# Norm gains of the three head groups folded into the rows of the output matrix, and gates loaded from DRAM into a buffer of their own

## The chip, the cores and the metric

One core of one Trainium2 chip runs the kernel. The metric is the device time of one launch in microseconds (us). In the profile, PE is TensorE, ACT is ScalarE, DVE is VectorE, POOL is GpSimd, and SP is SyncE, which here issues nearly all transfers.

## The reference, cut to what matters

A decoder layer on 1024 tokens of width 1024. Three head groups read one input projection: stick-breaking attention (4 heads x 64), gated DeltaNet (4 x 128, in chunks) and HGRN2 (4 x 64). Their outputs are normalised per head, two of them are gated, and all go through one output projection:

```
sb_o = rms_norm(sb_o, sb_gain)
dn_o = rms_norm(dn_o, dn_gain) * silu(split_heads(dn_z, DN_HEADS))
hg_o = rms_norm(hg_o, hg_gain) * sigmoid(split_heads(hg_g, HG_HEADS))
mix = concatenate([sb_o, dn_o, hg_o])          # widths 256, 512, 256
x = x + mix @ w_out
h2 = rms_norm(x, norm2)
ff = silu(h2 @ w_gate) * (h2 @ w_up)
return rms_norm(x + ff @ w_down, final_norm)
```

Each gain multiplies a column of `mix`, and a column of `mix` meets one row of `w_out`. All is float32; a product is three matmuls of high and low halves (high x high, low x high, high x low).

## The kernel before

The program is written by hand for each engine. Every engine has one list of instructions that it works off in order; semaphores (`wait_ge`, `then_inc`, and `reach`, which waits only for a positive count) join the lists. It has four parts: norm and first projections (to about 70 us), projection beside attention (to about 460 us), the mixer in steps t = 0 to 8 over chunks of 128 tokens (about 460 to 645 us), and output projection and feed-forward (to the end).

In step t of the mixer each engine works on several chunks: t (state, scores, outputs), u = t+1 (the inverse of a triangular matrix in seven levels, and the HGRN2 decays), v = t+2 (first products) and s = t-1 (transposes of finished rows). The places that matter:

- `gates` (POOL, L1996) multiplies the activated gates in `pb` by the gain row into `gate`, two instructions for each chunk, in front of `from_start` and `values` (both recorded at L1973, as most of POOL's work, the ten `spread` instructions too). `causal` begins POOL's next step and waits for DVE's `scores`.
- `final_sb`, `final_dn`, `final_hg` (DVE, recorded in the helper `final`, L1833) write `mix` by four instructions each: length factor times gate or gain. `queries(u, 0..6)`, `scores`, the adds of `update` and `low` are recorded at L1718, `with_decay` at L1820, `log_sigmoids` at L1769, `residual` at L1724, the two scans of `running` at L1779.
- `out_high` (ACT, L662) and `out_low` (POOL, L667) split a quarter of half of `w_out` into high and low halves. The first four (n = 0) stand at the end of steps 0 to 3, the other four (n = 1) behind the mixer. `inverse(u, lv)` (ACT, L1542) copies each turned level for PE's `update` (L1270).
- On PE: `turn` L1257, `pack` L1242, `new_values` L1326, `state_update` L1354, `key_key` L1376, `gated_out` L1396 and L1399, `key_query` L1383, `m_turn` L1408, `key_state` L1282, `out_product` L2107 to L2109.
- On SP, `load_rest(t)` brings a row block of 1280 columns (gates, HGRN2 values, attention output) into `pb`; `load_keys` and `load_queries` of chunk v stand behind it.

Of the kernel before, what the change touches and what calls it, by code (L numbers as in the profile page):

```python
# [13 lines left out]
P = 128  # L14
# [6 lines left out]
def trunk_program(nc, a, out):  # L21
# [91 lines left out]
    with ExitStack() as ctx:  # L113
# [27 lines left out]
        gain_row = sb("gain_row", [P, D])  # L141
        ssq = sb("ssq", [P, NT])
# [115 lines left out]
        pb = carve(TM - 2 * DNW)  # L258
        hv = pb[:, I_AT - 2 * DNW:I_AT - 2 * DNW + HGW]
# [21 lines left out]
        for name in """rows_loaded gains_loaded o_stored0 o_stored1 gr_loaded pa_loaded pb_loaded kt_loaded0 kt_loaded1 qt_loaded hin_loaded0 hin_loaded1  # L281
# [4 lines left out]
                qd at vb gated h_dl t_init qb h_bk kd  # L286
# [372 lines left out]
        def out_high(e, n, j):  # L659
            half, at = j // 2, 2 * (j % 2)  # L660
            e.wait_ge(sems["raw_loaded1" if half else "w_loaded0"], 16 * (len(ROWS) + n + 1 if half else (W_OUT + 1) // 2 + n + 1))
            e.activation(OUT_H[n][half][:, at:at + 2, :], OUT_RAW[half][:, at:at + 2, :], ACT.Copy).then_inc(sems["wh_ready"], 1)  # L662
# [495 lines left out]
        def mixer_sync(e):  # L1158
# [10 lines left out]
            def load_rest(c):  # L1169
                reach(e, "ho_done", c)  # L1170
                reach(e, "hs_done", c)
                reach(e, "gated", c)
                reach(e, "fin_sb", c)
                e.dma_start(pb[:, :], tm_dram[c * P:(c + 1) * P, 2 * DNW:]).then_inc(sems["pb_loaded"], 16)
# [39 lines left out]
            for t in range(NT + 1):  # L1214
# [5 lines left out]
                if live(t):  # L1220
                    load_rest(t)
                if t in (4, 5):
                    load_out(e, 1, t - 4)
# [316 lines left out]
        def mixer_act(e):  # L1540
# [102 lines left out]
            def step(t):  # L1643
# [11 lines left out]
                if live(u):  # L1655
                    inverse(u, 1)
                if live(u):
# [25 lines left out]
                if 0 <= t < 4:  # L1683
                    out_high(e, 0, t)
# [31 lines left out]
        def mixer_dve(e):  # L1716
# [120 lines left out]
            def final_dn(c):  # L1837
                e.wait_ge(sems["dn_r"], 2 * c + 2)
                e.wait_ge(sems["gated"], c + 1)
# [3 lines left out]
            def final_hg(c):  # L1843
                e.wait_ge(sems["hg_r"], 2 * c + 2)
                e.wait_ge(sems["gated"], c + 1)
# [3 lines left out]
            def final_sb(c):  # L1849
# [3 lines left out]
                final(c, SBH, pb[:, SB_AT - 2 * DNW:], r_sb[:, c, :], SBD, 0, gain_row[:, 0:SBW], "fin_sb")  # L1853
# [112 lines left out]
            e.wait_ge(sems["gains_loaded"], 16 * (SBH + DNH + 4))  # L1966
# [4 lines left out]
        def mixer_pool(e):  # L1971
# [17 lines left out]

            def gates(c):  # L1990
                e.wait_ge(sems["pb_loaded"], 16 * (c + 1))
                reach(e, "fin_hg", c)
                reach(e, "fin_dn", c)
                for at_, n in ((0, DNW), (DNW, HGW)):
                    src = pb[:, (Z_AT if at_ == 0 else G_AT) - 2 * DNW:]
                    ins = e.tensor_tensor(gate[:, at_:at_ + n], src[:, 0:n], gain_row[:, SBW + at_:SBW + at_ + n], ALU.mult)  # L1996
                ins.then_inc(sems["gated"], 1)
# [37 lines left out]
            def step(t):  # L2035
# [15 lines left out]
                if live(t):  # L2051
                    gates(t)
# [834 lines left out]
```

## Time and profile before

| | us |
|---|---|
| three runs | 1378.54, 1380.06, 1381.33 (median 1380.06) |
| the profiled execution | 1376.71 |
| its span | 1375.0 |
| PE busy | 1327.3 (97%) |
| DVE, POOL, ACT busy | 783.0, 674.8, 591.7 |

The span is the time from first to last instruction in the profile. Busy times overlap; which of them sets the end is read stage by stage.

### The profile page before, as it was taken

The page shows a single profiled execution, that of the slowest core. Times are in us where ns is not written, and L with a number is a line of the kernel's source. Part 1 is how long each engine was busy: PE and PEld are TensorE (multiplying, and loading weights), DVE is VectorE, ACT ScalarE, POOL GpSimd, SP SyncE. Part 2 cuts the span into 40 slices and gives each one's busy share as a digit, 9 for nine tenths or more (in the row PEclk, how much of TensorE's full clock was granted, in tenths as well). Part 3 has the DMA queues.
Part 4 walks back from the last instruction along what each step waited for, and adds up shares of the span by engine and source line. Part 5 has one row for each costly group of instructions (what it writes and reads, how often), then busy time and mean ns, then how long its engine had stood idle before and what let it go on. Part 6 is the DMA issues. An engine that isn't in the chain of part 4 may idle for free.

```text
span 1375.0 us, 24260 instructions
## 1 busy us (share of the span) xinstructions
PE 1327.3 (97%) x9101; PEld 1102.2 (80%) x9101; DVE 783.0 (57%) x1171; ACT 591.7 (43%) x1403; POOL 674.8 (49%) x583
## 2 busy tenths in 40 slices
PE   5999999999999888989999999999999999999997
PEld 4777887988878777777888788888888888888886
DVE  5014635557364588894148855555555556665657
ACT  6234445445343567552134333333333334444445
POOL 3234324143252577750401877667666677754442
PEclk9999999999999999989999999999999999999999
DMA  5131222323224433514200344445455445876663
GB/s 185 33 102 55 89 71 87 119 74 105 78 68 123 142 120 99 181 49 158 76 17 1 108 153 149 151 151 166 150 176 176 146 146 209 324 258 195 196 188 123
DMA packets 160371, 178.60 MB, mean 130 GB/s; under 512 B 9520, under 2 KB 110464, under 8 KB 160256
## 3 DMA queue, kind: packets, MB, share of 16 engines
q1 hardware_dynamic: 160112, 176.53, 40.4%
q8 instruction: 74, 1.21, 0.4%
q10 hardware_dynamic: 144, 0.52, 0.2%
q14 instruction: 41, 0.34, 0.1%
HBM read 124.32 MB, written 52.71 MB: 129 GB/s over the span
## 4 chain that ended last, share of the span: by engine, by line
PE 83%; DVE 5%; issue 3%; POOL 3%; ACT 3%; DMA 1%; SPq 0%; DVEq 0%; POOLq 0%; ACTq 0%
PE banks L2415 9%; PE banks L2416 9%; PE banks L2417 9%; PE banks L353 6%; PE banks L355 6%; PE banks L354 6%; PE banks L2426 4%; PE banks L2427 4%; PE banks L2428 4%; PE banks L692 2%; PE banks L693 2%; PE banks L694 2%; PE banks L2107 2%; PE banks L2109 2%; PE banks L2108 2%
## 5 line engine op out<-in xcount | busy, mean ns | idle before, releaser
L2573 POOL TENSOR_TENSOR w_l<-area,w_h 128x512 fp32r<-128x512 f32 x119 | 175.6, 1481 | 180.0 <-ACT w_h L2468 135.0
L2573 POOL TENSOR_TENSOR w_l<-w_raw,w_h 128x512 fp32r<-128x512 f32 x100 | 140.5, 1405 | 99.7 <-ACT w_h L2523 50.1
L353 PE MATMUL banks<-act_h,w_h 128*128 128x512 f32 x352 | 141.3, 402 | 0.0
L355 PE MATMUL banks<-act_h,w_l 128*128 128x512 f32 x352 | 137.5, 391 | 0.0
L354 PE MATMUL banks<-act_l,w_h 128*128 128x512 f32 x352 | 137.2, 390 | 0.0
L341 POOL TENSOR_TENSOR w_l<-w_raw,w_h 128x1024 fp32r<-128x1024 f32 x24 | 59.4, 2477 | 142.3 <-ACT w_h L334 125.1
L2415 PE MATMUL banks<-act_h,w_h 128*128 128x512 f32 x320 | 124.5, 389 | 0.0
L2416 PE MATMUL banks<-act_l,w_h 128*128 128x512 f32 x320 | 124.5, 389 | 0.0
L2417 PE MATMUL banks<-act_h,w_l 128*128 128x512 f32 x320 | 124.5, 389 | 0.0
L2426 PE MATMUL banks<-w_h,act_h 128*128 128x512 f32 x308 | 120.0, 390 | 0.3 <-DVE act_l L2725 0.3
L2428 PE MATMUL banks<-w_h,act_l 128*128 128x512 f32 x308 | 119.8, 389 | 0.0
L2427 PE MATMUL banks<-w_l,act_h 128*128 128x512 f32 x308 | 119.8, 389 | 0.0
L1018 POOL TENSOR_TENSOR area<-area 128x512 f32<-128x512 f32 (+3 forms) x48 | 50.4, 1050 | 109.8 <-DVE area L1037 109.8
L2415 PE MATMUL banks<-turns,w_h 128*128 128x512 f32 x240 | 93.5, 390 | 1.3 <-POOL w_l L2573 1.3
L2416 PE MATMUL banks<-turns,w_h 128*128 128x512 f32 x240 | 93.4, 389 | 0.0
L2417 PE MATMUL banks<-turns,w_l 128*128 128x512 f32 x240 | 93.4, 389 | 0.0
L1037 DVE TENSOR_TENSOR_SCAN area<-area,zeros 128x512 f32<-128x512 f32 (+3 forms) x48 | 53.3, 1110 | 68.2 <-ACT area L934 68.2
L1973 POOL TENSOR_TENSOR area<-area 128x128 f32<-128x128 f32 (+2 forms) x144 | 72.5, 533 | 38.5 <-ACT area L1542 17.1
L2725 DVE TENSOR_TENSOR act_l<-act_h 128x512 fp32r<-128x512 f32 x40 | 56.1, 1406 | 45.2 <-ACT act_h L2526 45.2
L2468 ACT ACTIVATE w_h<-area 128x512 fp32r<-128x512 f32 x84 | 52.4, 626 | 62.4 <-PE banks L2417 28.8
L353 PEld LDWEIGHTS banks<-act_h,w_h 128*128 128x128 f32 x352 | 66.1, 188 | 15.8 <-issue 2.8
L355 PEld LDWEIGHTS banks<-act_h,w_l 128*128 128x128 f32 x352 | 66.1, 188 | 14.3
(316 smaller groups left out, 3333.2 us busy)
## 6 DMA issues: line engine op xcount, KB each, us to landing
w_raw<-in_w_in SPq DMA_DIRECT2D x22, 512.0 KB, 4.1
w_raw<-in_w_gate SPq DMA_DIRECT2D x22, 512.0 KB, 4.6
area<-in_w_up SPq DMA_DIRECT2D x22, 512.0 KB, 4.7
ff_wide<-in_w_down SPq DMA_DIRECT2D x22, 512.0 KB, 4.3
down_sums<-ff_wide SPq DMA_DIRECT2D x11, 1024.0 KB, 4.1
area<-in_x SPq DMA_DIRECT2D x8, 1024.0 KB, 7.9
projected_tm<-area SPq DMA_DIRECT2D x32, 256.0 KB, 2.3
hidden_sums<-area SPq DMA_DIRECT2D x6, 1024.0 KB, 4.2
```

The source lines that it names most:

```text
L341: e.tensor_tensor(w_l[:, b], w_raw[:, b], w_h[:, b].bitcast(F32), ALU.subtract).then_inc(sems["wl_ready"], 1)
L353: e.matmul(dst, w_h[:, b, k], act_h[:, k, cols], start=(k == 0), stop=False)
L354: e.matmul(dst, w_h[:, b, k], act_l[:, k, cols], start=False, stop=False)
L355: mm = e.matmul(dst, w_l[:, b, k], act_h[:, k, cols], start=False, stop=(k == KT - 1))
L1973: e.tensor_tensor(dst, x, y, op).then_inc(sems[name], 1)
L2415: e.matmul(dst, slot(w_h, u)[:, k], hi[:, k, :], start=(opens and k == 0), stop=False, skip_group_check=True)
L2416: e.matmul(dst, slot(w_h, u)[:, k], lo[:, k, :], start=False, stop=False, skip_group_check=True)
L2417: mm = e.matmul(dst, slot(w_l, u)[:, k], hi[:, k, :], start=False, stop=(k == 3), skip_group_check=True)
L2426: e.matmul(dst, h, slot(w_h, u), start=(k == 0 and name not in ("p6", "p5", "p3")), stop=False, skip_group_check=True)
L2427: e.matmul(dst, h, slot(w_l, u), start=False, stop=False, skip_group_check=True)
L2428: return e.matmul(dst, l, slot(w_h, u), start=False, stop=(k == PAIRS - 1), skip_group_check=True)
L2573: e.tensor_tensor(slot(w_l, u), raw_use(u) if u < NU_FF else wd_raw(u - NU_FF), slot(w_h, u).bitcast(F32), ALU.subtract).then_inc(sems["fl ...
```

## The change

The four instructions of `final_sb` become one product with the length factors alone. POOL's `gates` go; `final_dn` and `final_hg` read a `gate` buffer that SP fills from DRAM by a transfer of its own, once both have finished with the chunk before. The gains are loaded as three columns with one value for each row of `w_out` (5 small transfers in place of 12), and `out_high` multiplies its two row blocks by them in place, one ACT instruction each, before it takes the high half. For n = 0 it moves from the end of the step to between `inverse(u, 1)` and `inverse(u, 2)`.

```diff
         def out_high(e, n, j):
...
+            if n == 0 and j == 0:
+                e.wait_ge(sems["gains_loaded"], 16 * (P // SBD + 1 + P // HGD))
+            for k in (at, at + 1):
+                first = (4 * half + k) * P
+                col = 0 if first < SBW else 1 if first < SBW + DNW else 2
+                ins = e.activation(OUT_RAW[half][:, k, :], OUT_RAW[half][:, k, :], ACT.Copy, scale=gain_cols[:, col:col + 1])
+            ins.then_inc(sems["w_scaled"], 1)
+            e.wait_ge(sems["w_scaled"], 4 * n + j + 1)
             e.activation(OUT_H[n][half][:, at:at + 2, :], OUT_RAW[half][:, at:at + 2, :], ACT.Copy).then_inc(sems["wh_ready"], 1)
...
             def load_rest(c):
                 reach(e, "ho_done", c)
                 reach(e, "hs_done", c)
-                reach(e, "gated", c)
                 reach(e, "fin_sb", c)
-                e.dma_start(pb[:, :], tm_dram[c * P:(c + 1) * P, 2 * DNW:]).then_inc(sems["pb_loaded"], 16)
+                e.dma_start(pb[:, :], tm_dram[c * P:(c + 1) * P, I_AT:]).then_inc(sems["pb_loaded"], 16)
+
+            def load_gates(c):
+                reach(e, "fin_dn", c)
+                reach(e, "fin_hg", c)
+                e.dma_start(gate[:, :], tm_dram[c * P:(c + 1) * P, Z_AT:I_AT]).then_inc(sems["gated"], 16)
...
                 if live(t):
                     load_rest(t)
+                    load_gates(t)
...
                 if live(u):
                     inverse(u, 1)
+                if 0 <= t < 4:
+                    out_high(e, 0, t)
                 if live(u):
                     inverse(u, 2)
...
                     whole_inverse(u)
-                if 0 <= t < 4:
-                    out_high(e, 0, t)
...
-                final(c, SBH, pb[:, SB_AT - 2 * DNW:], r_sb[:, c, :], SBD, 0, gain_row[:, 0:SBW], "fin_sb")
+                tt(mix[:, 0:SBW].rearrange("p (h d) -> p h d", d=SBD), attended.rearrange("p (h d) -> p h d", d=SBD),
+                   per_head(r_sb, c, SBH, SBD), ALU.mult, "fin_sb")
...
-            def gates(c):
-                e.wait_ge(sems["pb_loaded"], 16 * (c + 1))
-                reach(e, "fin_hg", c)
-                reach(e, "fin_dn", c)
-                for at_, n in ((0, DNW), (DNW, HGW)):
-                    src = pb[:, (Z_AT if at_ == 0 else G_AT) - 2 * DNW:]
-                    ins = e.tensor_tensor(gate[:, at_:at_ + n], src[:, 0:n], gain_row[:, SBW + at_:SBW + at_ + n], ALU.mult)
-                ins.then_inc(sems["gated"], 1)
...
-                if live(t):
-                    gates(t)
...
-            for first, n, width, name in ((0, SBH, SBD, "sb_gain"), (SBW, DNH, P, "dn_gain"), (SBW + DNW, 4, HGD, "hg_gain")):
-                for h in range(n):
-                    at = first + h * width
-                    e.dma_start(gain_row[:, at:at + width], a[name][0].partition_broadcast(P)).then_inc(sems["gains_loaded"], 16)
+            for col, width, name in ((0, SBD, "sb_gain"), (1, P, "dn_gain"), (2, HGD, "hg_gain")):
+                for at in range(0, P, width):
+                    e.dma_start(gain_cols[at:at + width, col:col + 1], a[name][0].rearrange("(p o) -> p o", o=1)).then_inc(sems["gains_loaded"], 16)
```

The waits on the gain row in front of the mixer go on DVE and POOL, and the waits behind the mixer name `fin_dn` and `fin_hg` in place of `gated` and `fin_sb`.

On ACT, step 0, from the copy of the new values to the copy of level 3, before (all of `inverse` is `area<-banks 128x256`):

```order
L1542 ACTIVATE area<-banks 128x512
L1542 ACTIVATE area<-banks 128x256 x2
L1542 ACTIVATE area<-area 128x256
L1609 ACTIVATE area<-area 128x768
L1542 ACTIVATE area<-area 128x128 x2
L1542 ACTIVATE area<-banks 128x256
```

The same place on ACT in the change, where the file's lines are some 14 further down:

```order
L1556 ACTIVATE area<-banks 128x512
L1556 ACTIVATE area<-banks 128x256
L668 ACTIVATE w_raw<-w_raw,gain_cols 128x512 x2
L671 ACTIVATE w_h<-w_raw 128x1024
L1556 ACTIVATE area<-banks 128x256
L1556 ACTIVATE area<-area 128x256
L1623 ACTIVATE area<-area 128x768
```

Three instructions stand between levels 1 and 2; before, one of them stood at the end of the step.

On POOL, the end of step 0 and the beginning of step 1, before: `decayed_keys`, `gates`, `from_start`, `values`, `out_low`, `causal`, `unit`:

```order
L1973 TENSOR_TENSOR area<-area,rest 128x512
L1996 TENSOR_TENSOR area<-area,gain_row 128x512
L1996 TENSOR_TENSOR area<-area,gain_row 128x256
L1973 TENSOR_TENSOR area<-area 128x256
L1973 TENSOR_TENSOR area<-area,vbs 128x512
L667 TENSOR_TENSOR w_l<-w_raw,w_h 128x1024
L1973 TENSOR_TENSOR area<-area,upto 128x512
L1973 TENSOR_TENSOR area<-ident,ones 128x256
```

The same in the change:

```order
L1987 TENSOR_TENSOR area<-area,rest 128x512
L1987 TENSOR_TENSOR area<-area 128x256
L1987 TENSOR_TENSOR area<-area,vbs 128x512
L676 TENSOR_TENSOR w_l<-w_raw,w_h 128x1024
L1987 TENSOR_TENSOR area<-area,upto 128x512
L1987 TENSOR_TENSOR area<-ident,ones 128x256
```

The two products of `gates` are gone, and all behind them moves up.

On SP, step 0 of the mixer in the change: `load_rows`, `load_rest`, `load_gates`, then `load_keys`, `load_queries` and `load_channels`:

```order
L1176 DMA area<-projected_tm 128x1024
L1182 DMA area<-projected_tm 128x512
L1187 DMA area<-projected_tm 128x768
L1192 DMA area<-projected_cm 128x4x128
L1197 DMA area<-projected_cm 128x4x128
L1205 DMA area<-projected_cm 128x6x128
```

Before, one transfer of 128x1280 stood in place of the second and third.

## Rows read from the trace of the kernel before

**Rows 1.** The page: span, and PE's busy tenths in 40 slices of 34.4 us.
```profile
span 1375.0 us, 24260 instructions
...
PE   5999999999999888989999999999999999999997
```
**Rows 2.** Windows: busy us of PE, PEld, DVE, ACT, POOL; clock, DMA share, GB/s.
```profile
500.00:600.00 100.00, 88.80 (x1760) 76.30 (x1759) 89.56 (x281) 66.76 (x225) 73.90 (x106) 1.00 0.42 134
```
**Rows 3.** POOL's timeline, end of step 1: start, duration, idle time ahead in brackets.
```profile
498.71 1.04 POOL L1973 TENSOR_TENSOR area<-area,rest 128x512 f32<-128x512 f32 x1 [1.98 <-PE banks L1354]
499.71 1.96 POOL L1996 TENSOR_TENSOR area<-area,gain_row 128x512 f32<-128x512 f32 x2
501.64 0.72 POOL L1973 TENSOR_TENSOR area<-area 128x256 f32<-128x256 f32 x1
502.32 1.09 POOL L1973 TENSOR_TENSOR area<-area,vbs 128x512 f32<-128x512 f32 x1
505.03 2.39 POOL L667 TENSOR_TENSOR w_l<-w_raw,w_h 128x1024 fp32r<-128x1024 f32 x1 [1.61 <-ACT w_h L662]
```
**Rows 4.** DVE's timeline in the same step.
```profile
496.81 0.86 DVE L1833 SCALAR_TENSOR_TENSOR area<-area,r_sb,gain_row 128x64 f32<-128x64 f32 x4
...
502.15 1.40 DVE L1718 TENSOR_TENSOR area<-area 128x128 f32<-128x128 f32 x2
503.48 1.11 DVE L1833 SCALAR_TENSOR_TENSOR area<-banks,r_dn,area 128x128 f32<-128x128 f32 x4
...
508.10 1.13 DVE L1724 SCALAR_TENSOR_TENSOR area<-banks,neg_d,area 128x128 f32<-128x128 f32 x4 [0.34 <-PE banks L1282]
```
**Rows 5.** ACT's timeline in steps 1 and 2.
```profile
502.24 0.63 ACT L1542 ACTIVATE area<-area 128x512 f32<-128x512 f32 x1
...
503.89 1.06 ACT L662 ACTIVATE w_h<-w_raw 128x1024 fp32r<-128x1024 f32 x1
...
512.13 0.38 ACT L1542 ACTIVATE area<-banks 128x256 f32<-128x256 f32 x1 [0.50 <-PE banks L1257]
514.80 0.38 ACT L1542 ACTIVATE area<-banks 128x256 f32<-128x256 f32 x1 [2.28 <-PE banks L1257]
```
**Rows 6.** PE, DVE and POOL timelines, end of step 4.
```profile
571.79 1.11 PE L1383 MATMUL banks<-area 128*128 128x128 f32 x8
...
569.48 1.39 DVE L1718 TENSOR_TENSOR area<-area 128x128 f32<-128x128 f32 x2
...
574.62 1.15 DVE L1769 SCALAR_TENSOR_TENSOR area<-area 128x256 f32<-128x256 f32 x1
...
574.22 1.27 POOL L1973 TENSOR_TENSOR area<-area,upto 128x512 f32<-128x512 f32 x1 [3.50 <-DVE area L1718]
```
**Rows 7.** DVE, POOL and PE timelines, step 6, and the windows view.
```profile
608.16 3.65 DVE L1833 SCALAR_TENSOR_TENSOR area<-area,r_sb,gain_row 128x64 f32<-128x64 f32 x4
...
608.05 2.00 POOL L1996 TENSOR_TENSOR area<-area,gain_row 128x512 f32<-128x512 f32 x2
...
612.40 0.65 PE L1270 MATMUL banks<-area 64*64 64x32 f32 x16 [2.46 <-DVE area L1718]
...
622.58 0.50 PE L2107 MATMUL banks<-w_h,act_h 128*128 128x512 f32 x1
...
612.40:622.50 10.10, 10.10 (x116) 8.95 (x116) 6.71 (x22) 3.02 (x14) 0.00 (x0) 0.53 0.19 60
```
**Rows 8.** PE's timeline, step 7, in front of the last scores.
```profile
634.78 0.43 PE L1314 MATMUL banks<-area 64*64 64x32 f32 x16 [1.50 <-DVE area L1791]
```
**Rows 9.** POOL and PE timelines behind the mixer: last halves of `w_out`, first use.
```profile
657.73 4.74 POOL L667 TENSOR_TENSOR turns<-area,turns 128x1024 fp32r<-128x1024 f32 x2
...
672.89 0.39 PE L2107 MATMUL banks<-w_h,act_h 128*128 128x512 f32 x1
```
**Rows 10.** SP's timeline, step 2: keys and queries of chunk 4.
```profile
508.09 0.37 SPq L1179 DMA_DIRECT2D area<-projected_cm  x1
515.07 0.37 SPq L1184 DMA_DIRECT2D area<-projected_cm  x1
```

More of the change, by code:

```diff
@@ L141, in trunk_program @@
         gain_row = sb("gain_row", [P, D])
+        gain_cols = sb("gain_cols", [P, 3])
         ssq = sb("ssq", [P, NT])
@@ L257, in trunk_program @@
         hstate = carve(2, P)
-        pb = carve(TM - 2 * DNW)
-        hv = pb[:, I_AT - 2 * DNW:I_AT - 2 * DNW + HGW]
+        pb = carve(TM - I_AT)
+        hv, attended = pb[:, 0:HGW], pb[:, HGW:]
         gate = carve(DNW + HGW)
@@ L285, in trunk_program @@
                 r xy tt hs_new f_log h_b h_sc e_cut act_low s_new h_qe h_fs m at0 fin_dn fin_hg fin_sb
-                qd at vb gated h_dl t_init qb h_bk kd
+                qd at vb gated w_scaled h_dl t_init qb h_bk kd
                 x1_ready gu_done ffh ffl down_done x_added out_ready out_stored
@@ L1838, in final_dn @@
                 e.wait_ge(sems["dn_r"], 2 * c + 2)
-                e.wait_ge(sems["gated"], c + 1)
+                e.wait_ge(sems["gated"], 16 * (c + 1))
                 reach(e, "mt_done", 2 * c)
@@ L1844, in final_hg @@
                 e.wait_ge(sems["hg_r"], 2 * c + 2)
-                e.wait_ge(sems["gated"], c + 1)
+                e.wait_ge(sems["gated"], 16 * (c + 1))
                 reach(e, "mt_done", 2 * c)
@@ L1965, in mixer_dve @@
             mix_dve(e, beside)
-            e.wait_ge(sems["gains_loaded"], 16 * (SBH + DNH + 4))
             e.wait_ge(sems["zeroed"], 4)
@@ L2082, in mixer_pool @@
                 e.memset(v, 0.0).then_inc(sems["zeroed"], 1)
-            e.wait_ge(sems["gains_loaded"], 16 * (SBH + DNH + 4))
             for t in range(NT + 1):
@@ L2140, in out_pool @@
             e.wait_ge(sems["ho_done"], NT)
-            e.wait_ge(sems["gated"], NT)
-            e.wait_ge(sems["fin_sb"], NT)
+            e.wait_ge(sems["fin_dn"], NT)
+            e.wait_ge(sems["fin_hg"], NT)
             for j in range(4):
@@ L2818, in _ @@
                 e.dma_start(x_sb[:, 2 * n:2 * n + 2, :], x_rows[:, 2 * n:2 * n + 2, :]).then_inc(sems[f"x_loaded{n}"], 16)
-            e.wait_ge(sems["fin_sb"], NT)
-            e.wait_ge(sems["gated"], NT)
             e.dma_start(gain_row[:, :], a["norm2"][0].partition_broadcast(P)).then_inc(sems["gain_loaded"], 16)
```

## The prediction

> **What bounds the kernel now.** I read the page first: in the slices from about 70 to 450 us and from 690 us to the end PE is busy nine tenths or more, and the hole lies between [rows 1]. Work of other engines in the full parts can move without moving the end. That settles the gain transfers: SP issues them at about 65 us, beneath a full PE, and five issues replace twelve. Price 0.
>
> Next the windows view of the hole. From 500 to 600 us PE is busy 88.8 of 100 us and DVE 89.6 [rows 2]. So neither is simply the limit: each step is a ring of some 22.4 us through both, and what lengthens DVE's list in the ring's serial part lengthens the step. POOL (73.9) and ACT (66.8) have room, and matter only where they make DVE or PE wait.
>
> Last the timelines of DVE and POOL side by side. A DVE product of two operands from SBUF stretches until the POOL instruction beside it ends. In step 6 the four `final_sb` instructions take 3.65 us instead of the 0.86 of step 1: they begin 0.1 us behind the two `gates` and end with POOL's `values` [rows 4, 7]. In step 1 the pair `queries(2)`, `queries(3)` takes 1.40 us and ends at the end of `values` (502.32 + 1.09 = 503.41), in step 4 it takes 1.39; alone the pair would take about 0.40 (a fifth of a us from start to start, as the 0.86 of four `final_sb` pieces shows) [rows 3, 4, 6]. DVE instructions with one operand in PSUM run at full speed beside the same POOL work: `final_dn`, 1.11 for four.
>
> The Trainium skill ("SBUF — State Buffer", Who interferes with whom) states it as a rule: a VectorE instruction with two SBUF inputs and a GpSimd instruction that reads SBUF lock each other out for a whole instruction, and the one issued first wins. The trace agrees with it in the 3.65 us above. The rule speaks for this change where `gates` go and against it where `out_low` moves up.
>
> **The change, part by part.** The sum is made against the profiled execution, 1376.71 us, which is 3.35 below the median of the runs, 1380.06.
>
> *Steps 4 and 5.* `gates` (1.96 us) leave POOL [rows 3], so `from_start` and `values` run 1.96 earlier and `values` has ended before `queries(2)` begins. The pair falls from 1.39 to 0.40: 0.99. `final_sb` becomes one product over 256 columns; I take 0.35 for it, so DVE has 0.45 less of it, of which PE's `state_update` in front of `update(5)` lets through about 0.28. Together 1.2 on DVE's list. But `scores` waits for `key_query` on PE, which runs from 571.79 to 572.90 and comes only 0.28 earlier [rows 6]; then `causal` and the `log_sigmoids` caught behind it (1.15, as now) follow at their present distance. With this limit 0.85 remains. Two steps: -1.7; bounds -0.6 (only the piece of `final_sb`) and -2.4 (no limit from PE).
>
> *Steps 0 to 3.* `out_low` now stands at 505.03 because it waits 1.61 us for `out_high` at the end of ACT's step [rows 3, 5]. With `out_high` moved up, it follows `values` at once: 499.71 + 0.68 + 1.08 = 501.5, and lasts 2.39, to 503.85. DVE reaches `queries(2)` at 502.15 - 0.28 = 501.87, inside it. The pair ends at about 504.1 where it now ends at 503.48 [rows 4]: +0.6. Against this, POOL now pays for `out_low` at 505.03 to 507.42, which makes `causal` and what is behind it late and pushes them onto DVE's two scans; with `out_low` gone from there about 0.5 comes back, an estimate, bounds 0 and 0.6. I take +0.1 for a step, +0.4 for four; bounds 0 and +2.4.
>
> *`out_high` between two levels.* ACT is idle 2.28 us in front of `inverse(u, 2)`: from 512.51 to 514.80 [rows 5]. Into it go two scalings of 128x512 and the 128x1024 copy. A 128x512 ACT instruction from SBUF to SBUF takes 0.63 and the copy 1.06 [rows 5]; the second scaling must have ended before the copy, so 0.53 + 0.63 + 1.06 = 2.2. It fits with 0.1 to spare. Behind ACT wait `high(s, 0)`, `from_start`, the first `spans`, `to_end` and `inverse(u, 3)`, and PE's `update` for the latter. Price 0; if scaling from a column were half as slow again, +0.5 a step, +2.0 in all. The matching copy at the end of the step is gone, where nobody waited for ACT.
>
> *Step 6.* `gates` go, so POOL has `from_start` at 608.05, to 608.75. The single `final_sb` product waits for that and ends at about 609.1; DVE is then free 2.7 us before the 611.8 that 608.16 + 3.65 gives now [rows 7]. PE sits idle 2.46 us in front of `update(5)` for exactly this [rows 7]: -2.5. Now the clock: in the 10.1 us behind that idle time the granted clock is 0.53 on average, so nearly all of it the lower level of 1.2 GHz, with PE busy throughout, while DVE has 6.71 us of work [rows 7]. Without the idle time I expect the clock of the steps before it, 1.00 [rows 2]. PE's work would then halve to about 5.4 us and DVE's 6.7 would set the pace: 10.1 - 6.7 = 3.4, of which I take 3.3. Bounds 0 and 3.4. Step 6: -5.8.
>
> On the clock the Trainium skill ("TensorE: Matmul & The Clock Gate", Terms) puts the penalty at the throttled time times one minus the clock ratio. A mean of 0.53 over 10.1 us means some 9.5 us at half clock; times one half that is 4.7, an estimate, and the sum below would be 1.4 lower; the rows' DVE time says less can be had.
>
> *Step 7.* PE idles 1.50 in front of its last `scores`, for DVE work that stands behind `final_sb` [rows 8]. That is alone on the port here and shrinks by 0.45: -0.45.
>
> *Transfers.* Bytes stay the same (512 + 768 columns for 1280). `load_gates(t)` waits for `final_hg(t-1)`, which stands behind `residual` (508.10) and two scans on DVE [rows 4], some 3 us after the keys' issue of now, 508.09; so `load_keys`, queued behind it, slips to about 511.8; `load_queries` goes at 515.07 as now, since it waits for POOL [rows 10]. Keys are wanted by `key_key` at the end of the step, 12 us later. `final_dn` wants the gates about 14 us after their issue. Price 0. If a landing came after its use, the excess would count in full in each step.
>
> *Behind the mixer.* Four `out_high` of 2.2 instead of 1.0 us on ACT. POOL's last `out_low` now ends at 657.73 + 4.74 = 662.5, and with POOL working 2.4 each it would end about 1.1 later; PE first reads those halves from 672.89 [rows 9]. Nine us of cover. Price 0.
>
> Sum: -1.7 + 0.4 - 5.8 - 0.45 = -7.55, that is 1369.2 for the profiled execution and 1372.5 on the median.
>
> **The rivals.**
>
> *The stall goes, the clock still falls.* What speaks for it: step 6 has little PE work left anyway (no products for a chunk 8), and small idle pieces stay. Then the 3.3 are missing: -4.25, 1375.8. Against it: PE would work from 609.9 without the idle 2.46 in front.
>
> *No change.* PE's dense part and `scores` hold steps 4 and 5 as they are, the insertion on ACT costs its 0.5 four times, the clock falls all the same, and only step 6 and 7 are left: -2.5 - 0.45 + 2.0 = about -1, 1379. For it speaks that ACT's gap fits with 0.1 to spare; against it, that PE waits for DVE in the ring, not the reverse, by DVE's 89.6 busy us [rows 2].
>
> *Slower.* `out_low` takes the port in the middle of the serial stretch in steps 0 to 3: DVE is held at `queries(2)`, `with_decay` comes late, and PE idles in front of `m_turn`. If that idle time drops the clock as in step 6, a step pays up to 3.4 more [rows 7]. Four times: +13.6 against -7.55, 1386. It decides from about three of the four steps on. Against it: by the sum PE's idle time grows by 0.6 only, far from 2.46.
>
> **How the numbers follow.** Chances: my forecast 0.50, the low clock 0.22, no change 0.15, slower 0.13. The likeliest gives 1372.5. Its own range is 1370 to 1375 by the bounds of its terms; the second case adds up to 1377. I give 1369 to 1378, which leaves out the slower rival and the upper half of no change. A measurement of this kernel tells 0.2%, 2.8 us: faster is below 1377.3, slower above 1382.8. The first case and nearly all of the second are faster, 0.71; 0.16 the same; 0.13 slower.
>
> **What would show it.** In the profile after: the step from `final_dn` to `final_dn` shorter by 0.85 in steps 4 and 5, and almost unchanged in 0 to 3; the `queries` pair at 0.4 in steps 4 and 5 and above 1.9 in steps 0 to 3; `inverse(u, 2)` not later behind `inverse(u, 1)`; no PE idle time of 2 us in step 6 and a clock of 1.00 behind it; DVE's `final_sb` at one instruction of 0.4, and near 1 in step 6. The prediction is wrong if `inverse(u, 2)` waits for the inserted copies, if the clock falls in steps 0 to 3, or if a new idle place takes over in step 6.

## The result, and the profile after

The changed kernel takes 1383.28 us, the median of 10 runs (1377.85 to 1389.55). The kernel before, run beside it, takes 1376.53 (10 runs, 1374.93 to 1381.33). The ratio is 1.0044, with a 95% interval of 1.0029 to 1.0059: slower by 0.4%, where 0.5% faster was forecast. A ratio here and below is an estimate of its own over all runs, not the quotient of the two medians. The profiled execution took 1382.94 us. The first lines of its page answer to [rows 1]:

```profile
span 1381.1 us, 24229 instructions
...
PE   5999999999999888898999999999999999999997
```

Taken as a whole the mixer shows nothing of the loss. These are POOL's timeline, DVE's and a row of PE's at the end of step 1, against [rows 3, 4]:

```profile
499.48 0.73 POOL L1987 TENSOR_TENSOR area<-area 128x256 f32<-128x256 f32 x1
500.16 1.04 POOL L1987 TENSOR_TENSOR area<-area,vbs 128x512 f32<-128x512 f32 x1
501.16 2.37 POOL L676 TENSOR_TENSOR w_l<-w_raw,w_h 128x1024 fp32r<-128x1024 f32 x1
507.24 1.27 POOL L1987 TENSOR_TENSOR area<-area,upto 128x512 f32<-128x512 f32 x1 [3.71 <-DVE area L1732]
```
```profile
501.65 2.23 DVE L1732 TENSOR_TENSOR area<-area 128x128 f32<-128x128 f32 x2
503.80 1.12 DVE L1847 SCALAR_TENSOR_TENSOR area<-banks,r_dn,area 128x128 f32<-128x128 f32 x4
```
```profile
506.61 0.68 PE L1422 MATMUL banks<-ident,area 64*64 64x64 f32 x16 [1.16 <-DVE area L1834]
```

The last row is PE's, at `m_turn`, which waits 1.16 us for the DVE work behind the pair; before, it waited 0.33 to 0.65 in these steps. `gates` is gone, `out_low` follows `values` at once, and DVE's `queries` pair lasts 2.23 us and ends 0.35 us behind `out_low`. Then POOL idles 3.71 us ahead of `causal`. In steps 4 and 5, which have no `out_low`, the pair takes 0.48 and 0.49.

ACT's timeline at the same place of step 2, against [rows 5]: two scalings and the copy follow `inverse(u, 1)`, and `inverse(u, 2)` comes right behind them.

```profile
511.64 0.89 ACT L1556 ACTIVATE area<-banks 128x512 f32<-128x512 f32 x2 [2.61 <-PE banks L1340]
512.42 1.32 ACT L668 ACTIVATE area<-area,gain_cols 128x512 f32<-128x512 f32 x2
513.78 1.06 ACT L671 ACTIVATE ff_h<-area 128x1024 fp32r<-128x1024 f32 x1
514.81 0.38 ACT L1556 ACTIVATE area<-banks 128x256 f32<-128x256 f32 x1
```

The group at 511.64 holds `new_values` and, last, `inverse(u, 1)`. It ends at 512.53, and with the 0.38 us of [rows 5] `inverse(u, 1)` began at 512.15. From there to `inverse(u, 2)` it is 2.66 us; in [rows 5] it was 2.67.

Step 6: `final_sb` is one DVE instruction, and there is no idle time of 2.46 us on PE and no low clock behind it as in [rows 7].

```profile
612.55 0.95 DVE L1732 TENSOR_TENSOR area<-area,r_sb 128x256 f32<-128x256 f32 x1
```

But step 5 has a new stall. PE's timeline shows one group of equal matmuls torn in two, with "issue" as what PE waited for; behind it the windows view (PE, PEld, DVE, ACT, POOL, clock, DMA share, GB/s) has the clock at 0.50 for 10.2 us:

```profile
585.50 0.41 PE L1328 MATMUL banks<-area 64*64 64x32 f32 x13
587.29 0.56 PE L1328 MATMUL banks<-area 64*64 64x32 f32 x19 [1.39 <-issue]
```
```profile
587.80:598.00 10.20, 10.20 (x108) 9.02 (x105) 7.68 (x25) 6.15 (x24) 2.72 (x3) 0.50 0.30 91
```

A table of the steps, measured from one `final_dn` to the next (the first of four DVE instructions each time), in us:

| step | 1 | 2 | 3 | 4 | 5 | 6 | 7 |
|---|---|---|---|---|---|---|---|
| before | 22.44 | 22.64 | 22.34 | 22.33 | 22.03 | 23.86 | 20.33 |
| after | 22.58 | 22.63 | 22.69 | 21.35 | 24.49 | 23.41 | 17.56 |

The sum is 154.71 against 155.97: the changed kernel leaves the mixer ahead. It still leads when the feed-forward begins. The first norm and the last addition into `gain_row` on DVE's timeline, of before and of after:

```profile
686.50 1.28 DVE L404 SCALAR_TENSOR_TENSOR ff_wide<-area,rstd,gain_row 128x1024 f32<-128x1024 f32 x1 [1.84 <-ACT rstd L379]
...
1155.25 0.68 DVE L2715 TENSOR_TENSOR gain_row<-gain_row,banks 128x512 f32<-128x512 f32 x1
```
```profile
685.75 1.28 DVE L405 SCALAR_TENSOR_TENSOR ff_wide<-area,rstd,gain_row 128x1024 f32<-128x1024 f32 x1 [1.83 <-ACT rstd L380]
...
1161.56 0.67 DVE L2717 TENSOR_TENSOR gain_row<-gain_row,banks 128x512 f32<-128x512 f32 x1
```

From 0.75 us ahead it falls to 6.31 behind. The stage between took 468.75 us and now takes 475.81: +7.06, in a part of the program that the change does not edit, where the clock is 1.00 in both and PE idles for the same 1.5 us between 690 and 1150 us (1.28 of them at 780). Only the distance from one matmul to the next differs. PE's timeline of before, then of after, at matmuls whose moving operand lies in `turns`, a block of SBUF behind the small tensors that holds moving operands of the gate and up products:

```profile
903.09 0.39 PE L2416 MATMUL banks<-turns,w_h 128*128 128x512 f32 x1
903.31 0.39 PE L2417 MATMUL banks<-turns,w_l 128*128 128x512 f32 x1
903.54 0.39 PE L2415 MATMUL banks<-turns,w_h 128*128 128x512 f32 x1
903.77 0.39 PE L2416 MATMUL banks<-turns,w_h 128*128 128x512 f32 x1
```
```profile
905.01 0.40 PE L2417 MATMUL banks<-turns,w_h 128*128 128x512 f32 x1
905.25 0.39 PE L2418 MATMUL banks<-turns,w_h 128*128 128x512 f32 x1
905.48 0.40 PE L2419 MATMUL banks<-turns,w_l 128*128 128x512 f32 x1
905.72 0.40 PE L2417 MATMUL banks<-turns,w_h 128*128 128x512 f32 x1
```

Three matmuls take 0.68 us from start to start there (903.09 to 903.77) and 0.71 here (905.01 to 905.72). Over all between 800 and 1100 us the mean is 226.7 ns before and 233.5 after. With `act_h` or `act_l` as moving operand it is 226.7 and 228.2, the excess lying in the first few behind a `turns` group. The busy time of 0.39 or 0.40 us, which overlaps with the next matmul's, hides this: it has to be read from the starts.

### The profile page after: what moved, and what is told of

Same layout as the page of the kernel before. It is cut to its first block, busy times and chain, and to the rows that moved or that the text cites. A ratio compares the mean times of both kernels' runs of the same rounds, so it can differ in the third digit from the quotient of the medians.

```text
span 1381.1 us, 24229 instructions
## 1 busy us (share of the span) xinstructions
PE 1332.8 (96%) x9101; PEld 1101.1 (80%) x9101; DVE 779.6 (56%) x1147; ACT 602.1 (44%) x1419; POOL 659.5 (48%) x567
## 4 chain that ended last, share of the span: by engine, by line
PE 87%; DVE 5%; POOL 3%; issue 3%; ACT 2%; DVEq 0%; POOLq 0%; ACTq 0%
PE banks L2417 9%; PE banks L2419 9%; PE banks L2418 9%; PE banks L354 6%; PE banks L356 6%; PE banks L355 6%; PE banks L2428 5%; PE banks L2430 5%; PE banks L2429 5%; PE banks L701 2%; PE banks L702 2%; PE banks L703 2%; PE banks L2109 2%; PE banks L2111 2%; PE banks L2110 2%
## 5 line engine op out<-in xcount | busy, mean ns | idle before, releaser
L2417 PE MATMUL banks<-turns,w_h 128*128 128x512 f32 x240 | 95.2, 397 | 1.3 <-POOL w_l L2575 1.3
L2418 PE MATMUL banks<-turns,w_h 128*128 128x512 f32 x240 | 94.7, 395 | 0.0
L356 PEld LDWEIGHTS banks<-act_h,w_l 128*128 128x128 f32 x352 | 66.1, 188 | 14.2
```

The source lines that it names most:

```text
L356: mm = e.matmul(dst, w_l[:, b, k], act_h[:, k, cols], start=False, stop=(k == KT - 1))
L2417: e.matmul(dst, slot(w_h, u)[:, k], hi[:, k, :], start=(opens and k == 0), stop=False, skip_group_check=True)
L2418: e.matmul(dst, slot(w_h, u)[:, k], lo[:, k, :], start=False, stop=False, skip_group_check=True)
```

## The experiments

```diff
-        gain_cols = sb("gain_cols", [P, 3])
+        gain_cols = sb("gain_cols", [P, 16])
```

> The changed kernel, with the three gain columns given 64 bytes of each partition in place of 12, so that everything allocated behind them, the operand buffers turns above all, starts at a multiple of 64 bytes again. Theory A (a start that is 32 bytes off a multiple of 64 slows each matmul whose moving operand is in turns from 226.7 to 233.5 ns): from 690 to 1150 us matmuls are 226.7 ns apart throughout, the 7.1 us lost there come back, 1376.2 us, ratio to before 0.998 to 1.001. Rival B (something else of the change, the order of transfers or the instruction list, slows them): 1383, ratio 1.004 as the change.

1376.52 us (12 runs), ratio 1.0004 (0.9984 to 1.0023). The `turns` matmuls are at 229.8 ns, neither 226.7 nor 233.5: a place that costs less, but not none. The ratio is the expected one by luck: the dense stage still loses 4.4 us, and in this profile steps 1 to 7 of the mixer take 151.0 us where before takes 155.97.

*The kernel before with an unused buffer of 32 bytes in the same place, and with one of 64.*

```diff
         gain_row = sb("gain_row", [P, D])
+        spare = sb("spare", [P, 8])
```

> The kernel before with nothing changed but an unused tensor of 32 bytes per partition behind gain_row. Theory A: turns starts 32 bytes off, matmuls on it are 233.5 ns apart, +7.1 us, ratio 1.005. Rival B: ratio 1.000.

1384.17 us (7 runs), ratio 1.0073 (1.0045 to 1.0100), `turns` matmuls at 233.5 ns. Nothing of the change is in this kernel but the 32 bytes, and it has the whole loss of the dense stage.

> The kernel before with an unused tensor of 64 bytes in the same place. Theory A: a multiple of 64 is kept, ratio 1.000, matmuls 226.7 ns apart. If any shift at all costs, or if 128 bytes is the measure, ratio 1.005.

1385.52 us (12 runs), ratio 1.0046 (1.0028 to 1.0064), 229.8 ns. So 64 bytes are not harmless, and theory A in the form "a multiple of 64 bytes is enough" falls: the spacing has more than two values.

*The padded kernel with `out_high` back at the end of ACT's step.*

```diff
                     inverse(u, 1)
-                if 0 <= t < 4:
-                    out_high(e, 0, t)
                 if live(u):
...
                     whole_inverse(u)
+                if 0 <= t < 4:
+                    out_high(e, 0, t)
```

> The padded change with out_high of the first half back at the end of the step, its two scalings with it. Theory C (out_low, moved up behind values, holds the read port in front of queries in steps 0 to 3): the pair of queries falls from about 2 us to 0.4 and each of the four steps shortens by 0.6 to 1.0, together 2.5 to 4 us less than with the padding alone, 1372.5 to 1374. Rival D (those steps are set by PE, and ACT's longer end of the step costs as much): within 1 us of the padded change.

1396.28 us (5 runs), ratio 1.0138 (1.0115 to 1.0161). The rows tell why. ACT's timeline, then DVE's, then PE's, end of step 1 and start of step 2:

```profile
511.19 1.33 ACT L668 ACTIVATE w_raw<-w_raw,gain_cols 128x512 f32<-128x512 f32 x2
512.55 1.06 ACT L671 ACTIVATE w_h<-w_raw 128x1024 fp32r<-128x1024 f32 x1
```
```profile
515.66 0.66 DVE L1783 SCALAR_TENSOR_TENSOR area<-area 128x256 f32<-128x256 f32 x1 [1.65 <-ACT area L1556]
```
```profile
517.61 0.43 PE L1284 MATMUL banks<-area 64*64 64x32 f32 x16 [2.03 <-DVE area L1732]
...
520.23 0.69 PE L1271 MATMUL banks<-ident,area 128*128 128x128 f32 x2 [0.99 <-DVE area L1732]
```

The block of 2.4 us stands ahead of `gated_squares` and `softplus`; DVE's `log_sigmoids` waits 1.65 us for the latter, and PE 2.03 for DVE; the granted clock falls for 6.8 to 10.2 us behind it in steps 2 to 4, and these steps take 26.2, 27.6 and 27.5 us. The copy of 1.06 alone had stood there before without this. Theory C is half right: the pair falls to 0.48 us, but the steps grow, because of what ACT delays. Of the two places tried for work of this length, the one between the levels, which the change chose, is the better.

**Which address counts.**

> The changed kernel with gain_cols allocated as 128 bytes per partition ([P, 32], of which 3 columns are used), so that every later tensor, turns among them, starts 128 bytes further on than in the kernel before. Theory A, sharpened by the runs before (start of turns at a multiple of 128 bytes: 227 ns per dense matmul; 64 bytes off: 230 to 231; 32 off: 234): the matmuls with turns as moving operand are back at 226 to 227 ns, the dense stage loses nothing against before, and the gain of the mixer (about 4 to 5 us in the padded run) stays to the end: 1371.5 to 1373.5 us, ratio 0.997. Rival B (the spacing is chance of the program's layout or something else that the change does in the dense stage): turns matmuls stay at 229 to 234 and the ratio stays at 1.000 or above.

1380.21 us (12 runs), ratio 1.0025 (1.0007 to 1.0043), 232.9 ns: the expectation of theory A missed.

> The kernel before with an unused buffer of 128 bytes per partition behind gain_row, nothing else. Theory A: turns matmuls at 227 ns, no change, ratio 1.000 within 0.002. Rival B: any further buffer slows the kernel, as those of 32 and 64 bytes did (ratios 1.0073 and 1.0046): ratio over 1.003.

1382.51 us (7 runs), ratio 1.0038 (1.0020 to 1.0055), again 232.9. By the letter of its text the rival "any further buffer slows the kernel" has this one.

*`turns` moved, with three small buffers behind it that hold no operand of these matmuls.* It lies inside the work area, behind `below`:

```diff
-        AREA = 25600
-        with nc.sbuf_tensor("below", [P, 10 * D], F32), ...
+        AREA = 25600 + 8
+        with nc.sbuf_tensor("below", [P, 10 * D + 8], F32), ...
...
         gs = carve(4, HALF)
+        carve(8)
```

> The kernel before with only turns and the three small views behind it (w_diff, raw_2, tmp_2) moved by 32 bytes; gain_row, the small tensors and the start of the work area stay where they were. Theory A with the moving operand as its cause: turns matmuls at 233 to 235 ns, act_h and act_l at 227, dense stage +6 us, 1382 to 1384 us, ratio 1.0045 to 1.006. Rival A2 (it is not turns' start but that of gain_row, the small tensors or the rest of the area that counts): turns matmuls stay at 227 and the ratio at 1.000.

1383.92 us (6 runs), ratio 1.0052 (1.0036 to 1.0068), 233.5 ns. `turns` itself counts; the small tensors in front of it do not.

*Everything moved by 32 bytes, and everything behind `gain_row` by 256:*

```diff
+        spare = sb("spare", [P, 8])
         act_h = sb("act_h", [P, KT, T], F32R)
```

> The kernel before with 32 unused bytes ahead of all tensors, so that the moving operands (act_h, act_l, turns), the stationary ones (w_h, w_l) and everything else start 32 bytes further on, and no distance between two tensors changes. Theory A1 (the distance between turns and the weights or other tensors counts): all dense matmuls at 227 ns, ratio 1.000. Theory A2 (the absolute address of the moving operand counts): those with turns at 234 ns and those with act_h and act_l, which were at 227 in every run so far, at about 234 too: dense stage +6 us for turns alone, some 10 to 14 us for all, ratio 1.007 to 1.010.

1376.86 us (12 runs), ratio 0.9995 (0.9980 to 1.0010), 226.7 ns. Theory A1 has it: `turns` starts 32 bytes further on than in before, as in the changed kernel, at no cost, since everything else has moved with it. PE's timeline at `turns`, 0.68 us for three again:

```profile
901.72 0.39 PE L2416 MATMUL banks<-turns,w_h 128*128 128x512 f32 x1
...
902.40 0.39 PE L2416 MATMUL banks<-turns,w_h 128*128 128x512 f32 x1
```

> The kernel before with an unused buffer of 256 bytes per partition behind gain_row: turns starts 256 bytes further on. Distances of 32, 64 and 128 bytes gave 234, 230 to 231 and 232 to 234 ns. If the spacing depends on the start within a unit of 256 bytes, the turns matmuls are at 227 ns and the ratio is 1.000; if on a longer unit or on the place itself, they stay above 229 ns, with a ratio of 1.002 or more.

1377.14 us (12 runs), ratio 0.9998 (0.9983 to 1.0013), 226.7 ns. 256 bytes are free, 32, 64 and 128 are not. So it is a distance, counted in units of 256 bytes. In the kernel before, `turns` minus `w_h` is 94720 bytes by the same count of tensor sizes, 370 times 256, and `act_h` and `w_l` too lie whole multiples of 256 from `w_h`. The next kernel asks whether the distance to the weights is the one. Between the two unused buffers it moves `w_h`, `w_l` and all that stands behind them up to `gain_row`:

```diff
         act_l = sb("act_l", [P, KT, T], F32R)
+        spare = sb("spare", [P, 8])
         w_h = sb("w_h", [P, 2, KT, P], F32R)
...
         gain_row = sb("gain_row", [P, D])
+        spare_2 = sb("spare_2", [P, 56])
```

> The kernel before with w_h, w_l and what lies behind them up to gain_row moved by 32 bytes, and everything behind gain_row by 256 bytes (which cost nothing by itself); act_h and act_l stay. If what counts is the distance, in units of 256 bytes, between a matmul's moving operand and its weights: all dense matmuls, those with act_h and act_l too, at 229 to 235 ns and a ratio of 1.007 to 1.010. If it is the distance of turns to act_h and act_l (which matmuls alternate with them), or to the small tensors, the dense matmuls stay at 227 ns.

1400.58 us (6 runs), ratio 1.0155 (1.0128 to 1.0182), more than expected. Now the matmuls with `act_h` and `act_l` are slow too, 233.3 ns, and so are those of the projections ahead of the mixer (233.3 for 228.0 between 300 and 440 us). PE's timeline:

```profile
920.25 0.40 PE L2417 MATMUL banks<-act_h,w_h 128*128 128x512 f32 x1
920.49 0.40 PE L2418 MATMUL banks<-act_l,w_h 128*128 128x512 f32 x1
920.72 0.40 PE L2419 MATMUL banks<-act_h,w_l 128*128 128x512 f32 x1
920.95 0.40 PE L2417 MATMUL banks<-act_h,w_h 128*128 128x512 f32 x1
```

One group in the same execution keeps its pace. In the second half of the output product `turns` is the moving operand and the weights lie in `act_h` and `act_l`, from which `turns` has moved by 256 bytes here and by 32 in the changed kernel. These matmuls are 227.6 ns apart in before, 233.4 in the changed kernel and 227.6 here:

```profile
709.66 0.39 PE L2109 MATMUL banks<-turns,act_h 128*128 128x512 f32 x1
...
710.34 0.39 PE L2109 MATMUL banks<-turns,act_h 128*128 128x512 f32 x1
```

So it is the distance between the two operands of a matmul, wherever they lie, and not that to a third tensor.

The stage from the first norm to the last addition into `gain_row`, in every profile, sorts without exception by this distance:

| kernels | moving operand minus weights, modulo 256 bytes | ns, `turns` | stage, us |
|---|---|---|---|
| before; all +32; +256; buffer behind the area (three kernels) | 0 | 226.7 | 468.7 to 468.8 |
| padded to 64; before +64; `out_high` last | 64 | 229.8 | 473.1 |
| 128 bytes (three kernels) | 128 | 232.9 | 474.5 |
| the changed kernel; before +32; `turns` +32 | 32 | 233.5 | 475.8 |
| weights +32 | 224, for all with weights in `w_h` and `w_l` | 233.3 | 479.9 |

The Trainium skill ("SBUF — State Buffer", Who interferes with whom) gives PE two SBUF read ports, one for the moving operand and one for the weight load, calls them independent, and says that PE never waits on anyone. No run here separates the ports, but two operands whose distance changes the pace by 3% are not independent in this kernel, and the measurement decides. That it is the weight load for the next matmul meeting the moving rows of this one is my reading; it was not measured by itself.

**The stall of step 5.** In steps 4 and 5 SP also loads the second half of the output matrix, 1 MB in each. In the changed kernel its issue stands behind the new `load_gates`, which waits for `final_dn` and `final_hg`.

```diff
                     load_rest(t)
-                    load_gates(t)
                 if t in (4, 5):
                     load_out(e, 1, t - 4)
+                if live(t):
+                    load_gates(t)
```

> The same as the run with 128 bytes, and on SP's queue the load of the output matrix's second half (steps 4 and 5) is issued ahead of the gates' load instead of behind it, so that it starts earlier in the step. Theory F: the stall of 1.39 us in the middle of a group of matmuls at 585 to 587 us in step 5, put down to issue, is TensorE waiting for its own instructions behind this 1 MB transfer; issued earlier, the transfer is over by then and the stall is gone: step 5 shorter by 1.4 us, 1371 us. Rival: the stall is independent of it and stays at the same matmul, with 1372.5 us.

1376.34 us (11 runs), ratio 0.9986 (0.9974 to 0.9997); the 128-byte kernel without it had 1.0025. The 1371 us expected are missed by 5, but the stall went as theory F has it: step 5 takes 22.11 us instead of 24.41, with a wait of 0.41 us for "issue" left at the same matmuls and no low clock. The cleaner pair is with the buffer out of the way:

```diff
-        gain_cols = sb("gain_cols", [P, 3])
...
         area = sb("area", [P, AREA])
+        gain_cols = sb("gain_cols", [P, 3])
```

> The changed kernel with gain_cols allocated behind the work area, as the last tensor, so that every other tensor, turns among them, starts exactly where it does in the kernel before. Theory A (the spacing of the dense matmuls follows from where turns starts, in whatever way): 226 to 227 ns with turns as moving operand, as in the kernel before, and the dense stage takes as long as before; the time is that of the run with 128 bytes less about 5 to 6 us: 1372 to 1376 us by whether a low clock follows the stall in step 5, ratio 0.996 to 0.999. Rival B (something that the change does makes these matmuls slower, not the place): 231 to 235 ns and a ratio of 1.002 or more.

1377.17 us (12 runs, 1370.99 to 1381.73), ratio 0.9979 (0.9961 to 0.9998), 226.7 ns. The ratio is in the expected range, but the median misses it by 1 us and equals that of before, 1377.18, so this gain is doubtful. The dense stage is back at 468.7 us: that was the question. SP's timeline and PE's in step 5 of this kernel:

```profile
584.58 0.32 SPq L1187 DMA_DIRECT2D area<-projected_tm  x1
584.96 0.43 SPq L658 DMA_DIRECT2D area<-in_w_out  x1
```
```profile
591.53 0.41 PE L1328 MATMUL banks<-area 64*64 64x32 f32 x13
593.32 0.56 PE L1328 MATMUL banks<-area 64*64 64x32 f32 x19 [1.39 <-issue]
```

> The same, with the load of the output matrix's second half issued ahead of the gates' load on SP's queue in steps 4 and 5. If theory F holds as in the run with 128 bytes (the 1.39 us stall of step 5 and the low clock behind it are gone, step 5 at 22.1 instead of 24.4 us), this is the fastest version: 1376.3 less 5.4 us that the dense matmuls lost there, 1370 to 1372 us, ratio 0.9945 to 0.996. If the effect there was chance, it equals the run without it.

1374.33 us (12 runs, 1370.04 to 1377.99), ratio 0.9962 (0.9945 to 0.9979). The load is issued ahead of the gates, and the group of 32 is whole:

```profile
577.01 0.43 SPq L658 DMA_DIRECT2D area<-in_w_out  x1
582.62 0.32 SPq L1187 DMA_DIRECT2D area<-projected_tm  x1
```
```profile
586.09 0.65 PE L1329 MATMUL banks<-area 64*64 64x32 f32 x32
```

Step 5 takes 21.23 us instead of 24.52, and the clock stays at 1.00 in it. Step 6 takes 21.56 instead of 23.36, since the 10.2 us of low clock behind the stall had reached into it. The median misses the expected 1370 to 1372 by 2 us; six of its twelve runs are at 1370.0 to 1372.6. What the stall is can be seen in part. The DMA view of the changed kernel from 577.0 to 584.6 has q1 alone, 1.69 MB; from 584.6 to 586.0, in which the last of the 1 MB lands (585.11), it has PE's next instructions too:

```profile
q1 hardware_dynamic: 1162, 1.69, 66.8%
```
```profile
q1 hardware_dynamic: 527, 0.26, 67.5%
q8 instruction: 1, 0.02, 4.9%
```

By the DMA records this packet of 16 KB starts 14.2 to 14.7 us after step 4's `final_dn` in the five kernels with the stall, and 12.1 to 12.8 in before and in the three with the early load. In the kernel with the buffer behind the area it starts at 590.96, and the load issued at 584.96 lands after 5.8 us, at 590.7. That PE's instructions queue behind a large load fits this; but the packet at 584.68 takes 1.10 us, and PE goes on only at 587.29, 1.5 us after its end, for which no view has a reason. The queueing itself is argued, the effect of the order on SP is shown, in both pairs of kernels.

**Why steps 0 to 3 give nothing.** In the kernels so far that place `out_high` as the change does, steps 2 and 3 take 22.6 to 22.7 us, and step 1 takes 22.6, or 22.8 to 23.0 where a low clock of the mixer's start runs into it; in the one with the early load the steps 4 to 6, without an `out_low`, take 20.8 to 21.6.

```diff
                 if 0 <= t < 4:
+                    e.wait_ge(sems["h_qe"], NX * (u + 1))
                     out_low(e, 0, t)
```

> The version with gain_cols behind the work area and the second load of the output matrix ahead of the gates, and one wait more: POOL's out_low in steps 0 to 3 waits for DVE's last queries product of the chunk (h_qe). In the version without it DVE's queries pair takes 2.0 to 2.2 us in steps 0 to 3, as long as the out_low beside it, and steps 0 to 3 last 22.6 us, where steps without an out_low last 20.8 to 21.2. Theory D (the port: out_low holds the pair, as the prediction had it, and that uses up what the removed gates give): the pair falls to 0.4, TensorE's idle time of 1.14 in front of m_turn shrinks, POOL has out_low done in its idle time of 3.7 us ahead of causal, steps 0 to 3 fall to 21 to 21.6 us, 1368 to 1371 us by the clock, ratio 0.992 to 0.994. Rival (something else holds steps 0 to 3, as the dense work of TensorE or ACT's list with the scalings): the pair shrinks and the steps stay at 22.6, ratio 0.996.

1366.96 us (6 runs, 1366.05 to 1375.26), ratio 0.9922 (0.9891 to 0.9953), the fastest kernel of the study, 1 us below what theory D expected. DVE's and POOL's timelines in step 1:

```profile
499.94 0.49 DVE L1733 TENSOR_TENSOR area<-area 128x128 f32<-128x128 f32 x2
500.33 1.13 DVE L1848 SCALAR_TENSOR_TENSOR area<-banks,r_dn,area 128x128 f32<-128x128 f32 x4
```
```profile
498.44 1.04 POOL L1988 TENSOR_TENSOR area<-area,vbs 128x512 f32<-128x512 f32 x1
502.14 2.37 POOL L676 TENSOR_TENSOR w_l<-w_raw,w_h 128x1024 fp32r<-128x1024 f32 x1 [2.65 <-DVE area L1733]
504.46 1.28 POOL L1988 TENSOR_TENSOR area<-area,upto 128x512 f32<-128x512 f32 x1
```

The pair is at 0.49, `out_low` fills the idle time ahead of `causal`, and steps 1 to 3 take 21.51, 21.85 and 21.52 us. Step 4 takes 21.52, where it took 20.82 without the wait: a step counted from a `final_dn` that the stretched pair has delayed, to one that it has not, comes out short. The time from the start of the profile to step 4's `final_dn` is free of this. In three kernels with no low clock in the mixer up to there it is 569.57 us (before with 128 bytes), 569.04 (128 bytes and the early load) and 565.22 (with the wait). So the wait added to POOL is worth 3.8 us, 0.3% of the kernel. The ratios, 0.9962 and 0.9922, say 0.4, but their intervals just overlap; of the runs at a mean clock of 0.993 or more, those without the wait took 1370.0 to 1372.6 us, those with it 1366.05 to 1367.40.

## Why the prediction was wrong, point by point

**The step that failed** is none of its terms but one it did not have. The sum has terms for the mixer alone; what lies behind it is settled under *Behind the mixer* with "Nine us of cover. Price 0", and everything after that was held unchanged because no instruction there changes. The new buffer's 32 bytes changed it: +7.06 us in the profile, +0.5 to +0.7% when added alone (ratios 1.0073 and 1.0052). The second failure is that of *Transfers*, below, 5.1 us. From the forecast -7.55 the two lead to +4.6; the profiled executions differ by +6.23, and the rest is spread over the points below.

**The base and the range.** The forecast of 1372.5 stands on a median of three runs, 1380.06; ten runs of before gave 1376.53, on which the same sum would have been 1369.0. And the bounds of its terms add up to 1371.3 and 1375.6, not to the 1370 and 1375 that it states. Neither decides: the measured time lies above them all.

**Transfers.** The prediction followed the keys behind the gates on SP's queue, rightly to no cost, but not `load_out`, which the queue has there in steps 4 and 5 only. Its delay goes with the 1.39 us stall and a low clock of 10.2 us: 3.3 us in step 5 (24.52 against 21.23) and 1.8 in step 6 (23.36 against 21.56). So its last sign of being wrong, a new idle place, came true, though in step 5 and not in step 6.

**Steps 4 and 5.** -0.85 a step forecast, by the `queries` pair falling to 0.40 and PE's `key_query` as the limit. The pair fell to 0.48; step 4 gave -0.98 in the changed kernel, and -0.81 in the kernel with the wait, the one whose step 4 neither begins nor ends with a stretched pair. Step 5 gave -0.80 there and in the kernel with the early load; with 128 bytes and the early load it gave +0.08, 0.41 us of "issue" among it. So the term is right in size. The 20.82 us of step 4 in other kernels are not the early load's doing, since the 128-byte kernel with the late load has them too; the changed kernel's 21.35 has a wait of 0.36 us for "issue" in it that those lack. That PE's `key_query` is the limit was not tested.

**Steps 0 to 3.** +0.1 a step forecast; +0.14, -0.01 and +0.35 measured in steps 1 to 3. The mechanism too was as written: the pair lasts as long as `out_low` beside it, here 2.23. What it left unsaid is that this swallows a gain: with `out_low` out of the pair's way the same steps give 0.8 to 0.9 each, as much as the forecast had for steps 4 and 5.

**A reading that its rows do not show.** For DVE instructions with one operand in PSUM at full speed beside POOL work it names `final_dn`, 1.11 for four. But POOL is idle there: `values` ends at 503.41, `out_low` begins at 505.03, and `final_dn` runs from 503.48 to 504.59 [rows 3, 4]. The statement holds by another row: `residual`, 1.13 us for four at 508.10 [rows 4], has POOL busy beside it all the time, and takes 1.13 at 622.1 us too, where POOL does nothing. No term rests on it.

**`out_high` between two levels.** Price 0, and so it was. The estimate of 2.2 us for scalings and copy measured 2.42 (512.42 to 514.84), and still `inverse(u, 2)` came as soon behind `inverse(u, 1)` as before.

**Step 6 and 7.** -5.8 and -0.45 forecast. The 2.46 us idle time and the low clock are gone, as the forecast had it and as its rival "the clock still falls" had not. In the kernel without the stall of step 5 the two steps give -2.30 and -2.79 against before: -5.1 for the forecast -6.25. The low clock of before ran over the end of step 6 (611.7 to 621.9), so part of its gain shows in step 7. Its length is not fixed: in the seven kernels that are before with unused buffers it is 6.8 to 13.7 us, and the two steps together take 43.8 to 45.8 us, where this profile of before has 44.2. The size of this term is known to no better than about 1 us. PE's own idle time there shrank from 1.50 [rows 8] to 1.38 only, so the term of 0.45 was mostly not there.

**The sum.** Steps 1 to 7 take 149.19 instead of 155.97, -6.8, in the kernel with the buffer behind the area and the early load; the forecast was -7.55. Its ratio of 0.9962 is -5.2 us. Part of the difference lies behind the mixer, where PE waits up to 2.4 us for "issue" at the first `out_product`, and 0.59 in the profile of before. The row is the changed kernel's:

```profile
641.20 0.61 PE L1353 MATMUL banks<-ident,area 128*128 128x128 f32 x4
644.22 0.47 PE L2109 MATMUL banks<-w_h,act_h 128*128 128x512 f32 x1 [2.41 <-issue]
```

A wait of 1.9 to 2.7 us is there in most kernels, those that are before with an unused buffer among them, and in three it is 0.6 to 0.8; what decides it stays open. In the time little of it shows: from the last `final_dn` to the first norm before takes 49.49 us, 2.0 of them at half clock, and the changed kernel 49.82, all at full clock. The kernel with the early load takes 51.31, and there the clock is at 0.50 for 3.4 us behind the wait.

**The slower rival** named the right sign and the wrong mechanism. It had `out_low` drop the clock in steps 0 to 3. PE's idle time in front of `m_turn` did grow, from 0.33 to 0.65 us to 1.16, but no low clock followed in steps 1 to 3.

## What to carry to other kernels

A new tensor, however small, moves every tensor behind it. In a kernel bound by dense matmuls, compare the start addresses of moving operands and weights before and after a change, keep their distance a multiple of 256 bytes as here, and put small new buffers behind the large ones.

Work taken off an engine lets what stood behind it start earlier, on that engine and on the DMA queue alike, and the new neighbour may cost what was saved. The change as written lost 0.4%. With its buffer out of the way and the load issued early it gained 0.4%, and a wait that sent the freed work back to a place where no DVE product stood against it made that 0.8%.

When a change loses time in a part it does not touch, compare starts of equal instructions there before looking for waits.

## What the runs showed of the hardware that was not expected

- The pace of 128x512 fp32r matmuls depends on the distance from moving operand to weights modulo 256 bytes: 226.7 ns at 0, 229.8 at 64, 232.9 at 128, 233.5 at 32. With 128 the starts alternate between 229 and 238 ns.
- The granted clock is 0.50 at the start of the mixer (from 464 to 469 us) for 3.4 us in three profiles and 17 to 24 us in eight, with and without the change; one has 6.8 us from 486.8, and four have no such stretch. It accounts for much of the spread of runs: of the twelve of the kernel with the early load, six at a mean clock of 0.986 to 0.988 took 1376.0 to 1378.0 us and six at 0.993 to 0.999 took 1370.0 to 1372.6.
- The stall of 1.39 us in step 5 came with 10.2 us at half clock in three kernels; in the one padded to 64 bytes the same stall had none behind it, and step 5 took 22.91 us instead of 24.4 to 24.5. With `out_high` last it is 1.66 us, with 6.8 at half clock.
